# Residual with tokens on partitions, handed over by token block, in a two-layer hybrid encoder trunk

## What is computed

```python
for l in range(DEPTH):                                   # DEPTH = 2
    f = swiglu(rms_norm(x, ffn1_pre_g[l]), ffn1_w_gate[l], ffn1_w_up[l], ffn1_w_down[l])
    x = x + 0.5 * rms_norm(f, ffn1_post_g[l])
    m = hybrid_mixer(rms_norm(x, mix_pre_g[l]), cos, sin, w_in[l], ...)
    x = x + rms_norm(m, mix_post_g[l])
    f = swiglu(rms_norm(x, ffn2_pre_g[l]), ffn2_w_gate[l], ffn2_w_up[l], ffn2_w_down[l])
    x = x + 0.5 * rms_norm(f, ffn2_post_g[l])
# rms_norm(x, g) = x * rsqrt(mean(x*x over features) + 1e-6) * g
# swiglu(x, wg, wu, wd) = (silu(x @ wg) * (x @ wu)) @ wd, inner width 2816
```

## Time and profile before

| | us |
|---|---|
| median of 3 runs | 2079.45 (2075.5 to 2079.79) |
| span of the profiled execution | 2078.5 |
| PE busy | 2020.5 (97%) |
| DVE busy | 897.6 (43%) |
| ACT busy | 693.5 (33%) |
| POOL busy | 179.4 (9%) |
| mean granted TensorE clock | 0.982 of full |

### The profile page before, as it was taken

How to read it: one execution, slowest core, us unless ns; L and a number is a source line. 1 busy time by engine, 2 the same in 40 slices (tenths; PEclk the granted TensorE clock), 3 DMA queues, 4 the chain that set the end, 5 groups by cost and what they waited for, 6 DMA issues and landing times.

```text
span 2078.5 us, 25293 instructions
## 1 busy us (share of the span) xinstructions
PE 2020.5 (97%) x9540; PEld 1628.4 (78%) x9540; DVE 897.6 (43%) x1137; ACT 693.5 (33%) x901; POOL 179.4 (9%) x185
## 2 busy tenths in 40 slices
PE   7999999999999999999999999999999999999997
PEld 6888888696677888888778888886956778888885
DVE  3444422635445544431364444226354464444314
ACT  5322211524443423221252223124444343223212
POOL 2000000202222000000020000003032220000000
PEclk9999999999999999999999999999999999999998
DMA  4222222230012222222212222223200112222222
GB/s 165 102 83 98 101 101 92 90 109 21 1 42 81 82 101 99 85 98 101 102 62 102 86 96 101 101 95 115 72 11 21 41 61 102 101 101 93 89 101 81
DMA packets 26615, 176.01 MB, mean 85 GB/s; under 512 B 3330, under 2 KB 3492, under 8 KB 6308
## 3 DMA queue, kind: packets, MB, share of 16 engines
q1 hardware_dynamic: 25024, 170.03, 22.4%
q10 hardware_dynamic: 1508, 4.87, 0.7%
HBM read 172.79 MB, written 2.10 MB: 84 GB/s over the span
## 4 chain that ended last, share of the span: by engine, by line
issue 77%; PE 16%; POOL 5%; DVE 1%; ACT 1%; DMA 0%; POOLq 0%; SPq 0%; DVEq 0%; ACTq 0%
POOL xL L1474 3%; PE ps L365 2%; PE ps L367 2%; PE ps L366 2%; PE ps L600 1%; PE ps L707 1%; POOL rstd L1484 1%; PE ps L725 1%; PE ps L518 1%; PE ps L519 1%; PE ps L520 1%; PE ps L714 0%; PE ps L609 0%; PE ps L641 0%; PE ps L682 0%
## 5 line engine op out<-in xcount | busy, mean ns | idle before, releaser
L1115 DVE TENSOR_TENSOR WL<-raw,WH 128x2048 fp32r<-128x2048 f32 x152 | 348.3, 2292 | 722.7 <-ACT WH L836 722.7
L365 PE MATMUL ps<-xH,WH 128*128 128x512 f32 x1632 | 639.3, 392 | 0.0
L367 PE MATMUL ps<-xH,WL 128*128 128x512 f32 x1632 | 635.4, 389 | 0.0
L366 PE MATMUL ps<-xL,WH 128*128 128x512 f32 x1632 | 635.3, 389 | 0.0
L836 ACT ACTIVATE WH<-raw 128x2048 fp32r<-128x2048 f32 x156 | 298.8, 1915 | 675.1 <-PE ps L367 675.1
L367 PEld LDWEIGHTS ps<-xH,WL 128*128 128x128 f32 x1632 | 306.1, 188 | 64.8
L365 PEld LDWEIGHTS ps<-xH,WH 128*128 128x128 f32 x1632 | 306.1, 188 | 64.4 <-issue 1.0
L366 PEld LDWEIGHTS ps<-xL,WH 128*128 128x128 f32 x1632 | 306.2, 188 | 63.8 <-issue 1.0
L366 PE MATMUL ps<-hL,WH 128*128 (+1 forms) x704 | 273.9, 389 | 0.0
L367 PE MATMUL ps<-hH,WL 128*128 (+1 forms) x704 | 273.9, 389 | 0.0
L365 PE MATMUL ps<-hH,WH 128*128 (+1 forms) x704 | 273.9, 389 | 0.0
(11 more groups left out here) (224 smaller groups left out, 1712.4 us busy)
## 6 DMA issues: line engine op xcount, KB each, us to landing
raw<-stream SPq DMA_DIRECT2D x158, 1024.0 KB, 4.8
x<-x_in SPq DMA_DIRECT2D x4, 512.0 KB, 9.7
wq<-w_q_up ACTq DMA_DIRECT2D x4, 512.0 KB
out<-x SPq DMA_DIRECT2D x8, 256.0 KB, 2.1
const<-consts ACTq DMA_DIRECT2D x2, 578.5 KB
wkv<-w_kv_up ACTq DMA_DIRECT2D x2, 512.0 KB
cos<-positions ACTq DMA_DIRECT2D x2, 256.0 KB
gains_all<-gains_in SPq DMA_DIRECT2D x1, 79.5 KB, 4.9
```

The source lines that it names most:

```text
L365: mm(dst, wh, xh, start=start, stop=False)
L366: mm(dst, wh, xl, start=False, stop=False)
L367: return mm(dst, wl, xh, start=False, stop=stop)
L1115: tt(WL[:, slot, :], raw[:, slot, :], WH[:, slot, :].bitcast(F32), ALU.subtract).then_inc(wL_ready, 1)
```

## The change

x lies with tokens on partitions: four blocks of 128 tokens by 1024 features. The down products exchange their operands (`down_tile`): a block of 128 tokens of `hH` or `hL` is stationary, 512 columns of `WH` or `WL` move, and banks 2b and 2b+1 hold block b of the result. Their count and width stay.

A mean of squares now lies along the free axis. ACT squares with an accumulated sum (`square_f`, `square_x`), DVE adds eps (`average_f`, `average_x`), POOL raises one column per block to -0.5 (`root_f`, `root_x`), and DVE applies scale and gain at once, from gain rows that are broadcast to all partitions (`norm_g`, two more DMAs of SP per stage). The new x block is normalised fully before the stage (`normed`), turned by eight transposes on PE into the two banks of its block (`turn_block`), and split from PSUM by ACT (`high_x`) and DVE (`low_x`). So the column sums, the spreads, the scaling of each gate and up tile and the `busy` products go.

```diff
+def slot_of(i):
+    return 2 if i == 0 else (i - 1) % 2
...
+            def turn_block(stage, b):
+
+                pe.wait_ge(xn_ready, BLK * stage + b + 1)
+                for t in range(DT):
+                    last = nc.tensor.transpose(ps[:, 2 * b + t // 4, t % 4 * P:(t % 4 + 1) * P],
+                                               xn[:, b % 2, t * P:(t + 1) * P], ident[:])
...
+                turn_block(stage, 2)
+                turn_block(stage, 3)
+                for p, slot, banks, width in ((base, 2, (0, 1), (P, P)), (base + 1, 0, (2, 3), widths)):
+                    wait_pair(p)
+                    pe.wait_ge(xH_ready, BLK * stage + 4)
+                    pe.wait_ge(xL_ready, BLK * stage + 4)
+                    whole_pair(slot, banks, width).then_inc(pair_done, 1)
...
+                def last_pairs(stage, p, slots, held):
+
+                    wait_pair(p)
+                    wait_pair(p + 1)
+                    for d in range(2 * BLK):
+                        if stage < STAGES - 1 and d == 6:
+                            turn_block(stage + 1, 0)
+                        last = down_tile(slots[0], d, held[0], False, False)
+                        if d == 2 * BLK - 1:
+                            last.then_inc(pair_done, 1)
+                        down_tile(slots[1], d, held[1], False, True).then_inc(f_ready, 1)
+                    if stage < STAGES - 1:
+                        turn_block(stage + 1, 1)
...
+                    last_pairs(stage, base + FT + 9, (0, 1), (hidden(18), hidden(20)))
...
+                def high(p, m, raw_slot, slot):
+
+                    act.wait_ge(landed[raw_slot], 16 * (m + 1))
+
+                    act.wait_ge(pair_done, p - 1)
+                    af(WH[:, slot, :], raw[:, raw_slot, :], ACT.Copy).then_inc(wH_ready, 1)
...
+                def residual(stage, b):
+
+                    if b == 0:
+                        dve.wait_ge(norm_g_landed, 16 * min(2 * stage + 1, 2 * STAGES))
+                    dve.wait_ge(rstd_f_ready, BLK * (stage - 1) + b + 1)
+                    dve.wait_ge(x_ready, BLK * (stage - 1) + b)
+                    link(stt(step[:].rearrange("p (a i) -> p a i", a=2), ps[:, 2 * b:2 * b + 2, :], rstd_f[:, b:b + 1],
+                             norm_g[:, 0, :].rearrange("p (a i) -> p a i", a=2), ALU.mult, ALU.mult))
+                    tt(x[:, b, :], x[:, b, :], step[:], ALU.add).then_inc(x_ready, 1)
...
+                    if stage == 0 and b == 0:
+                        dve.wait_ge(norm_g_landed, 16)
+                    dve.wait_ge(rstd_x_ready, BLK * stage + b + 1)
+                    if b >= 2:
+                        dve.wait_ge(x_turned, BLK * stage + b - 1)
+                    stt(xn[:, b % 2, :], x[:, b, :], rstd_x[:, b:b + 1], norm_g[:, 1, :], ALU.mult,
+                        ALU.mult).then_inc(xn_ready, 1)
```

More of the change, by code:

```diff
@@ L353, in _ @@
+            for b in range(BLK):
+                sp.wait_ge(x_ready, BLK * (STAGES - 1) + b + 1)
+                sp.dma_start(out[:, b, :], x[:, b, :]).then_inc(out_stored, 16)
+            sp.wait_ge(out_stored, 16 * BLK)
         @block.tensor
@@ new lines, in whole_pair, with enter @@
+            def whole_pair(slot, banks, widths):
+                for k in range(DT):
+                    for j in range(2):
+                        at = j * SLAB + k * P
+                        last = three(ps[0:widths[j], banks[j], :], wH(slot)[:, at:at + widths[j]],
+                                     wL(slot)[:, at:at + widths[j]], xH[:, k, :], xL[:, k, :],
+                                     k == 0, k == DT - 1)
+                return last
+            def enter(stage, base, widths=(P, P)):
+                if stage == 0:
+                    turn_block(0, 0)
+                    turn_block(0, 1)
+                turn_block(stage, 2)
[5 more added lines that the diff above has]
+                    whole_pair(slot, banks, width).then_inc(pair_done, 1)
@@ L400, in tiles_pair @@
+            for layer in range(DEPTH):
+                due = counter(layer)
+                def tiles_pair(p, slot, banks, middle=None):
+                    wait_pair(p)
+                    for k in range(DT):
+                        if k == DT // 2 and middle is not None:
                             middle()
@@ L428, in down_tile, with down_pair @@
                                      first and j == 0, last_pair and j == 1)
-                    if last_pair and d != F_ORDER[-1]:
-                        last.then_inc(f_ready, 1)
-                    return last
-                def down_pair(p, slot, moving, first, last_pair, order=F_ORDER, scaled=None):
-                    pe.wait_ge(wH_ready, due(wH_ready, p + 1))
-                    pe.wait_ge(wL_ready, due(wL_ready, p + 1))
+                    return last
+                def down_pair(p, slot, held, first, order=range(2 * BLK), emptied=None):
+                    wait_pair(p)
@@ L506, in pair, with mixer @@
+                    down_pair(base + FT, slot_of(FT), hidden(0), True, order=FFN_START, emptied=n0 + FT)
+                    down_pair(base + FT + 1, slot_of(FT + 1), hidden(2), False)
+                    for n in range(2, 9):
+                        down_pair(base + FT + n, slot_of(FT + n), hidden(2 * n), False)
+                    last_pairs(stage, base + FT + 9, (0, 1), (hidden(18), hidden(20)))
+                def mixer(stage, base):
                     def pair(i, banks, **kw):
-                        tiles_pair(base + i, (slot + i) % 2, banks, **kw)
+                        tiles_pair(base + i, slot_of(i), banks, **kw)
@@ new lines, in high_next, with square_f @@
+                def high_next(stage, base, i):
+                    act.wait_ge(landed[(base + i) % 2], 16 * ((base + i) // 2 + 1))
+                    if stage:
+                        act.wait_ge(f_ready, 2 * BLK * stage)
+                    af(WH[:, slot_of(i), :], raw[:, (base + i) % 2, :], ACT.Copy).then_inc(wH_ready, 1)
+                def square_f(stage, b):
+                    for d in (2 * b, 2 * b + 1):
+                        act.wait_ge(f_ready, 2 * BLK * (stage - 1) + d + 1)
+                        if b:
+                            act.wait_ge(sum_f_ready, 2 * BLK * (stage - 1) + d - 1)
+                        af(squares[:, 0, d % 2 * SEQ:(d % 2 + 1) * SEQ], ps[:, d, :], ACT.Square,
+                           scale=1.0 / (32.0 * SHARES[(stage - 1) % 3]),
+                           accum_out=sum_f[:, d:d + 1]).then_inc(sum_f_ready, 1)
@@ new lines, in square_x, with high_x @@
+                def square_x(stage, b):
+                    if stage:
+                        act.wait_ge(x_ready, BLK * (stage - 1) + b + 1)
+                    else:
+                        act.wait_ge(x_landed[b], 16)
+                    if b:
+                        act.wait_ge(sum_x_ready, BLK * stage + b)
+                    af(squares[:, 1, :], x[:, b, :], ACT.Square, scale=1.0 / 32.0,
+                       accum_out=sum_x[:, b:b + 1]).then_inc(sum_x_ready, 1)
+                def high_x(stage, b):
+                    act.wait_ge(x_turned, BLK * stage + b + 1)
+                    af(block_of(xH, b), turned_block(b), ACT.Copy).then_inc(xH_ready, 1)
@@ L1201, in ffn @@
[L1201 to L1209 removed]
+                        dve.wait_ge(hL_ready, n)
```

791 lines of the change are left out of this document (356 added, 435 removed).

## The result

The changed kernel takes 2155.4 us in the median against 2079.5 us: the ratio is 1.0373, with a 95% interval of 1.0358 to 1.0388. That is 75.9 us slower; the prediction had 2144 us, 11 us less. The profiled execution spans 2153.3 us against 2078.5.

The account below looks back on a forecast made before the run. PE, busy 97% of the span, was taken as the bound, so only its time without useful products could change: 2078.5 + 71 - 9.7 + 6 - 13.9 + 11.9 = 2143.8, put as 2144 us, range 2112 to 2168.

Parts of the forecast that it names:

- start, second pair later: Program start: loading, normalising and turning x's blocks puts the end of the first pair at 39.7 against 27.8 us, +11.9.
- five hand-overs: Between stages: PE loses 28.7 us instead of 14.5 at each, +14.2 us five times, +71 in all.
- column sums and spreads gone: Small products inside six stages: column sums of 0.81 us and as many products for the spread vanish, -9.7 us.
- exchanged operands of the down pairs: Down products inside stages: the same count of products with stationary and moving operands exchanged costs nothing, 0 us.
- Wait for weights: Before a stage's last two down pairs: PE waits for ACT's copy and DVE's subtraction into a just-read slot, 4.5 us.
- The cold products behind it: Last two down pairs: the weights' wait may lower PE's clock, 1.5 us taken, bounds 0 and 3.4.
- Block 0: Inside the last two down pairs: PE waits 0.8 us for this block's normalisation and turns it for 1.0, 1.8 us.
- The chain behind the last product: Hand-over: single waits through DVE's order until all four blocks are split, 18.4 us before the next stage's first products.
- First products cold: Start of the next stage: products go at half rate for 5 us behind the gap, costing 2.5 us per hand-over.
- rival (c): Hand-over chain: POOL's three single powers take 3.0 us each instead of 0.53, 7.4 us more per hand-over; 2181 us, chance 0.07.
- Rival (a): Waits for weights and transposes: PE's clock holds at full through them, 26 us less, 2118 us; chance 0.12.
- Rival (b): Hand-overs: overlap by blocks works, only block 3's chain follows the last product, 16.3 us each; 2077 us, chance 0.06.

Follow-up runs that it names:

- third_slot: Changed kernel with the last weight pair of each stage put into the third slot: 2112.3 us, ratio 1.0165 to the kernel before.
- block2_first: Changed kernel with DVE's residuals of blocks 2 and 3 ahead of the subtraction that splits block 1: 2132.9 us, ratio 1.0266 to the kernel before.
- three_placed: Changed kernel with last pair in third slot, residual of block 2 ahead of block 1's subtraction, and 160 unused bytes ahead of hH: 2078.2 us, ratio 1.0010.
- placed_h: Changed kernel with 160 unused bytes ahead of hH, nothing else: 2138.9 us, ratio 1.0301 to the kernel before.
- aligned_h: Changed kernel with 32 unused bytes ahead of hH, nothing else: ratio 1.0341 to the kernel before.
- three_edits: Changed kernel with last pair in third slot, residual of block 2 ahead of block 1's subtraction, and 32 unused bytes ahead of hH: 2087.9 us, ratio 1.0054.

## Why the prediction was right, and where it was not

By its own steps, against the two profiles (spans 2078.5 and 2153.3 us):

| step | predicted, us | measured, us |
|---|---|---|
| start, second pair later | +11.9 | +11.4 (27.77 to 39.12) |
| five hand-overs, 14.5 to 28.7 each | +71 | +70.6 (28.1 to 29.7 each) |
| last stage's wait and the end | +6 - 13.9 | -6.8 |
| column sums and spreads gone | -9.7 | -13 |
| exchanged operands of the down pairs | 0 | +13 |

*The mechanism holds.* Wait for weights 4.5 us: 4.48 in all six stages, and third_slot took it away. The cold products behind it: 1.5 taken, 2.3 measured in the mean, inside the bounds of 0 and 3.4. The reason given for 1.5, that part of the cold time passes in the wait, holds for little of it: the clock fell at 372.3, and the wait ended at 373.45 (window below). Block 0: a wait of 0.8 and 1.0 for turning predicted; no wait was measured, and the turning cost 1.1 (from the product at 392.69 to the one at 393.98, 1.29 us instead of 0.23, with the next one late by 0.1). The chain behind the last product: 18.4 predicted, 17.6 measured, in the order that was written down; block2_first shows that DVE's order made it. First products cold: 2.5 predicted, the first pair took 12.4 to 13.9 us instead of 10.9, 2.6 more in the mean.

```profile
372.00:373.00 1.00, 0.00 (x0) 0.00 (x0) 1.00 (x1) 0.78 (x1) 0.00 (x0) 0.63 0.00 0
```

*Part of the agreement is luck.* The hand-over was 4.5 + 1.5 + 1.8 + 18.4 + 2.5 = 28.7 in the prediction, and it is 4.6 + 2.3 + 1.1 + 17.6 + 2.6, with 0.5 for slow down products in the last pairs, 28.7 in the measured mean: two terms too large by 0.7 and 0.8 stand against one too small by 0.8 and one that was missing.

*POOL*, rival (c): a power of one column takes 0.55 us, 0.53 were estimated. At the start one took 1.55 us beside DVE's normalisation from two SBUF tensors; none of those in the chain of a hand-over did. The Trainium skill, "GPSIMD Engine Reference", Specifications, names contention with DVE instructions that have two SBUF inputs, and the trace agrees: in that row DVE had begun 0.15 us before the power. Where it began 0.07 us after the power (18.16), the power took 0.55 us.

*Rival (a)*, the clock holds, is refuted by every hand-over above. *Rival (b)*, no slower, would have needed both things it named, a free slot and the residual of block 2 further ahead; three_placed has both, loses 16.6 to 17.9 us in a hand-over where (b) had 16.3, and stands at 1.0010.

*The step that failed* is one sentence in the first paragraph: "adding the same count of products with exchanged operands costs nothing". The exchange does cost nothing, but the small tensors that came with the change moved hH by 672 bytes, to a place where each of 2112 down products with the weights takes 0.0076 us more: 16.1 us, 13.1 of them in the nine single down pairs of four stages (36 x 0.365) and the rest in the last pairs, which the hand-over's row contains. The prediction named the row in which it would show (a spacing of the down products other than 0.227), but gave it no price. The second miss goes the other way: the products for sums and spreads that vanish were worth 13, not 9.7. The gate and up part of a feed-forward stage became 1.9 us shorter where 1.6 were counted, since a place was worth 0.94 us instead of the 0.81 of the one that was priced. The mixers became 3.7 and 2.2 us shorter, but this is a soft number: between kernels whose mixer is the same it took 223.8, 225.4 or 227.1 us (block2_first, changed kernel, placed_h), and the kernel before has 229.0 and 227.7 for its two. The other rows of the table differ by 0.3 us in sum, and together this is the difference of 9.5 between the predicted span, 2143.8, and 2153.3. The rest of the 11 us is the step from span to run: the profiled run took 2155.2 us, 1.9 more than its span, where the prediction named 1 and, in putting 2144, left it out.

## What to carry to other kernels

A hand-over by blocks only overlaps if the orders let it: look for the engine whose program order puts an item whose inputs are early behind one whose inputs are late, and for the buffer that the interleaved last tiles still share. Work of the next stage that needs only part of the input is worth more in the gap than a shorter chain, even cut into halves. And when a tensor is added or removed, compare the distances between the operands of the main products, or their spacing in the trace: a multiple of 256 bytes and 16 bytes to either side of it were free here, the other distances tried cost 1.0 to 3.4%, and one measurement with both operands moved by 16 bytes does not follow this.

## What the runs showed of the hardware

The spacing of products of 512 columns depends on the distance between stationary and moving operand in SBUF, modulo 256 bytes: 0.2267 us at 0, 0.2290 at 192, 0.2325 at 128, 0.2332 to 0.2334 at 32, 64, 160 and 224, 0.2343 at 96. A padding of 32 bytes slowed the kernel before by 0.8%.

The time at 1.2 GHz behind a wait is not fixed. In aligned_h the spell at the first wait for weights lasted about 3.4 us (371.7 to 375.1), in the changed kernel, with the same wait of 4.48 us, 6.8 (372.3 to 379.1). The row of aligned_h in which it ends:

```profile
374.20:375.20 1.00, 1.00 (x4) 0.81 (x3) 0.06 (x1) 0.00 (x0) 0.00 (x0) 0.53 0.93 377
```

And the full clock can come back behind transposes alone. In three_edits PE did nothing but 16 transposes from 399.48 to 403.5, after 6.45 us without work. The clock rose at about 403.9, before any product:

```profile
403.00:403.50 0.50, 0.47 (x3) 0.06 (x1) 0.50 (x1) 0.00 (x0) 0.00 (x0) 0.50 0.00 0
403.50:404.00 0.50, 0.00 (x0) 0.00 (x0) 0.27 (x1) 0.50 (x1) 0.00 (x0) 0.64 0.00 0
404.00:404.50 0.50, 0.00 (x0) 0.00 (x0) 0.00 (x0) 0.50 (x2) 0.00 (x0) 1.00 0.00 0
```

It was lost again at 407.3, behind the 2.46 us wait for the last split. In the last microsecond before the first product the clock was at 1.00 in three of the five hand-overs of three_edits, in three of three_placed and in one of aligned_h. In block2_first, with the same 6.45 us, the same transposes and the same 2.46 us, it was at 0.50 in all five, as in the changed kernel: what decides is not shown. The prediction quoted the Trainium skill, "TensorE: Matmul & The Clock Gate", Part 4, PE-mode transpose, by which the full clock doesn't engage for transposes. The trace agrees for the transposes of blocks 2 and 3 in the hand-overs of the changed kernel, which ran at half clock (16 in 3.98 us), and not in the rows above, where the rise has nothing but transposes ahead of it; the measurement decides. Those of blocks 0 and 1, among products or right behind them, ran at full clock (8 in 1.04 us).
